# Layer 0's gates, branch and output projections as three products of high and low halves

## The reference

```python
def merge_branches(o_na, o_hg, hg_gate, gate_na, gate_hg, hg_gain, w_na_o, w_hg_o, w_out):
    y_na = from_heads(o_na) @ w_na_o
    y_hg = gated_head_norm(o_hg, hg_gate, hg_gain) @ w_hg_o
    return (jax.nn.sigmoid(gate_na) * y_na + jax.nn.sigmoid(gate_hg) * y_hg) @ w_out

# in parallel_mixer, for latent and context rows alike
(na_q, na_k, na_v, hq, hf, hb, hi, hg, ga, gh) = split_columns(h @ w_in)   # ga, gh: the two gates, 1024 columns each
# in reference, per layer
x = x + g1 * y_lat                                 # residual with the output projection
f = grouped_moe(...)                               # 16 experts, top-2 inside the best of 4 groups
```

## Time and profile before

| | |
|---|---|
| time, median of 3 runs | 1708.45 us (1707.89 to 1711.21) |
| the profiled execution's own time | 1708.12 us |
| its span | 1706.3 us |
| PE busy | 1538.7 us (90%) |
| DVE busy | 765.9 us (45%) |
| ACT busy | 571.5 us (33%) |
| POOL busy | 233.4 us (14%) |
| mean granted clock of the PE | 0.956 of full speed |

### The profile page before, as it was taken

The page is one execution under the profiler, slowest core; times in us unless marked ns, Lnnn a source line. Parts: engine busy times, 40 slices in busy tenths (PEclk is TensorE's granted clock), DMA queues, the critical chain, the costliest instruction groups (busy, mean ns, idle before and its releaser), DMA issues.

```text
span 1706.3 us, 15944 instructions
## 1 busy us (share of the span) xinstructions
PE 1538.7 (90%) x6246; PEld 913.2 (54%) x6246; DVE 765.9 (45%) x1047; ACT 571.5 (33%) x759; POOL 233.4 (14%) x204
## 2 busy tenths in 40 slices
PE   3999999999999995999999739999988996999885
PEld 1444665454444433788888525466547884443332
DVE  3045871666101125888888551665283114111103
ACT  3223431354000115787877442232142013111101
POOL 0005962200000001111110010074310000000000
PEclk9999999999999996999999959999998998999998
DMA  9411106498122223899999921112661445999992
GB/s 360 173 50 50 40 13 191 156 386 302 49 99 99 99 74 148 290 397 401 400 398 401 349 98 57 42 51 81 166 247 48 150 148 187 395 393 395 395 393 85
DMA packets 167139, 352.05 MB, mean 206 GB/s; under 512 B 21776, under 2 KB 22928, under 8 KB 167056
## 3 DMA queue, kind: packets, MB, share of 16 engines
q1 hardware_dynamic: 145472, 331.52, 52.2%
q0 software_dynamic: 3456, 12.58, 2.0%
q10 hardware_dynamic: 18128, 6.82, 2.0%
HBM read 339.38 MB, written 11.53 MB: 206 GB/s over the span
## 4 chain that ended last, share of the span: by engine, by line
PE 83%; DVE 6%; DMA 3%; issue 3%; ACT 2%; POOL 1%; SPq 0%; DVEq 0%; POOLq 0%; ACTq 0%
PE bank L501 20%; PE bank L512 6%; PE bank L1007 6%; PE bank L554 5%; PE bank L703 5%; PE bank L691 5%; PE bank L1029 4%; PE bank L790 3%; PE bank L784 3%; PE bank L781 3%; PE bank L578 2%; PE bank L472 2%; PE bank L814 2%; PE bank L1040 2%; PE bank L819 2%
## 5 line engine op out<-in xcount | busy, mean ns | idle before, releaser
L501 PE MATMUL bank<-hT,ring 128*128 128x512 f32 (+1 forms) x1024 | 371.1, 520 | 11.5 <-ACT hT L1330 6.4
L501 PEld LDWEIGHTS bank<-hT,ring 128*128 128x128 f32 x1024 | 197.0, 193 | 179.9 <-issue 160.7
L2233 DVE TENSOR_TENSOR slab_lo<-slab,high 128x4096 fp32r<-128x4096 f32 x48 | 212.0, 4420 | 6.8 <-ACT high L1517 6.2
L1517 ACT ACTIVATE high<-slab 128x4096 fp32r<-128x4096 f32 x48 | 174.1, 3632 | 23.0 <-PE bank L790 13.1
L1007 PE MATMUL bank<-narrow_slab,picked 128*64 128x512 f32 x256 | 114.4, 600 | 11.6 <-issue 11.4
L1778 POOL DMA_INDIRECT feed_rows<-token_table,slot_token x16 | 42.0, 2628 | 555.5 <-DVE slot_token L2173 360.5
L1008 PE MATMUL bank<-narrow_slab,picked 128*64 128x512 f32 x256 | 114.6, 601 | 0.0
L512 PE MATMUL bank<-ring,hT 128*128 128x512 f32 x256 | 110.5, 592 | 0.0
L554 PE MATMUL bank<-hT,ring 128*128 128x512 f32 (+1 forms) x256 | 104.8, 548 | 0.0
L1485 ACT ACTIVATE gsig<-bank 128x512 f32<-128x512 f32 (+1 forms) x32 | 15.7, 491 | 214.9 <-PE bank L501 214.9
L703 PE MATMUL bank<-merged,ring 128*128 128x512 f32 (+1 forms) x256 | 83.1, 486 | 2.6 <-DVE merged L2094 2.6
(11 more groups left out here) (260 smaller groups left out, 2249.2 us busy)
## 6 DMA issues: line engine op xcount, KB each, us to landing
ring<-in_w_ada SPq DMA_DIRECT2D x24, 2048.0 KB, 15.7
ring<-in_w_in SPq DMA_DIRECT2D x24, 2048.0 KB, 9.2
slab<-in_w_gate SPq DMA_DIRECT2D x16, 2048.0 KB, 14.7
slab<-in_w_up SPq DMA_DIRECT2D x16, 2048.0 KB, 14.9
slab<-in_w_down SPq DMA_DIRECT2D x16, 2048.0 KB, 14.7
narrow_slab<-in_w_gate SPq DMA_DIRECT2D x16, 2048.0 KB, 18.0
narrow_slab<-in_w_up SPq DMA_DIRECT2D x16, 2048.0 KB, 22.0
narrow_slab<-in_w_down SPq DMA_DIRECT2D x16, 2048.0 KB, 19.3
```

The costliest lines, as they stand in the source:

```text
L501: mm = T.matmul(o[:, lo:TOK], w[:, k, c * P:(c + 1) * P], hT[:, k, lo:TOK], start=(k == 0), stop=(k == KT - 1))
L1517: S.activation(high[kind][:], w[:], ACT.Copy)\
L2233: V.tensor_tensor(low[:], w[:], high[kind][:].bitcast(f32), ALU.subtract)\
```

## The change

In layer 0 the operands of the gate, branch and output projections are split into a high half (a copy to float32r, on ACT) and a low half (the rest, on DVE), and each float32 matmul becomes three float32r ones. Layer 1 keeps the old code.

- Weights are split by chunks of 128 output columns: `gate_high(n)`/`gate_low(n)` (1024 elements a row), `way_high`/`way_low` for the branches (512), `out_high`/`out_low` (1024). The high halves have two buffers of each kind; the low half overwrites the chunk in its ring slot.
- `hT` is split during attention: high halves of tiles 2 to 7 on ACT in steps p = 4 to 9, low halves over `hT` itself on DVE in steps 6 to 11; tiles 0 and 1 after attention. `ona`, `oh` and `merged` are split likewise.
- The head norm is taken in among the gates: the four sums (`head_squares`) stand between the PE's first products, the roots get four buffers (`ors`, `ors_more`), and DVE scales one head in each of the steps n = 1 to 4.
- The first two output chunks are prepared in steps 14 and 15; the rest beside the output projection.
- The fill of gate 0's slab waits for all 16 merges instead of the first, since its place now holds high halves.

The core of the diff (of `way_high`, `out_high`, `way_low`, `out_low` and `merged_high` only the use is shown; they are built as `gate_high` and `gate_low` are, a chunk waiting for the product that read its buffer two chunks before):

```diff
-merged = fixed("merged", [P, KT, TOK], offset=B0)
+merged = fixed("merged", [P, KT, TOK], offset=A0 + 32 * KB)
+ors_more = fixed("ors_more", [P, 2, TOK], offset=B0 + 36 * KB)
+hT_hi = fixed("hT_hi", [P, KT, TOK], f32r, offset=B0)
+hT_lo = fixed("hT_lo", [P, KT, TOK], f32r, offset=hT_at)
+ona_lo = fixed("ona_lo", [P, 4, TOK], f32r, offset=A0 + 24 * KB)
...
+gate_hi = [fixed(f"gate_hi{i}", [P, KT, P], f32r, offset=B0 + (24 + 4 * i) * KB) for i in range(2)]
+way_hi = [fixed(f"way_hi{i}", [P, 4, P], f32r, offset=B0 + (32 + 2 * i) * KB) for i in range(2)]
+out_hi = [fixed(f"out_hi{i}", [P, KT, P], f32r, offset=A0 + (16 + 4 * i) * KB) for i in range(2)]
...
+def gate_chunk(n):
+    br, d = n // KT, n % KT
+    key = ("in", 0, (8, 10)[br] + d // 4)
+    return key, chunk_of(slot(key), KT, d % 4), chunk_of(slot_low(key), KT, d % 4), gate_hi[n % 2]
+def way_chunk(n):
+    br, d = n // KT, n % KT
+    key = (("nao", "hgo")[br], 0)
+    return key, chunk_of(slot(key), 4, d), chunk_of(slot_low(key), 4, d), way_hi[n % 2]
...
+def wide_gates():
+    first = [2, 3, 4, 5, 6, 7, 0, 1]
+    for n in range(16):
+        br, d = n // KT, n % KT
+        key, _, low, high = gate_chunk(n)
+        o = open_bank(key + (d % 4,), "gate_sig")
+        pe.wait_ge(sem["chunk_high"], n + 1)
+        for i, k in enumerate(first):
+            if n == 0 and k in (2, 0):
+                pe.wait_ge(sem["tile_high"], (8, 0, 6)[k])
+            T.matmul(o[:, :], high[:, k, :], hT_hi[:, k, :], start=(i == 0), stop=False)
+        for i, k in enumerate(first):
+            if n == 0 and k in (2, 0):
+                pe.wait_ge(sem["tile_low"], (8, 0, 6)[k])
+            T.matmul(o[:, :], high[:, k, :], hT_lo[:, k, :], start=False, stop=False)
+        pe.wait_ge(sem["chunk_low"], n + 1)
+        for k in range(KT):
+            mm = T.matmul(o[:, :], low[:, k, :], hT_hi[:, k, :], start=False, stop=(k == KT - 1))
+        mm.then_inc(sem["psum_ready"], 1)
+        if d % 4 == 3:
+            slot_spent[slot_of(key)] = (sem["psum_ready"], jobs[0])
+        if n == 0:
+            head_squares(0)
+            head_squares(1)
+        key, _, low, high = way_chunk(n)
+        x_hi, x_lo = ((ona_hi, ona_lo), (oh_hi, oh_lo))[br]
+        o = open_bank(("y", l, br, d), "merged_ready")
+        pe.wait_ge(sem["way_high"], n + 1)
+        if d == 0:
+            pe.wait_ge(sem["head_high"], 4 * br + 4)
+        for k in range(4):
+            T.matmul(o[:, :], high[:, k, :], x_hi[:, k, :], start=(k == 0), stop=False)
+        if d == 0:
+            pe.wait_ge(sem["head_low"], 4 * br + 4)
+        for k in range(4):
+            T.matmul(o[:, :], high[:, k, :], x_lo[:, k, :], start=False, stop=False)
+        pe.wait_ge(sem["way_low"], n + 1)
+        for k in range(4):
+            mm = T.matmul(o[:, :], low[:, k, :], x_hi[:, k, :], start=False, stop=(k == 3))
+        mm.then_inc(sem["psum_ready"], 1)
+        if d == KT - 1:
+            slot_spent[slot_of(key)] = (sem["psum_ready"], jobs[0])
+        if n == 0:
+            head_squares(2)
+            head_squares(3)
+def wide_out():
     for d in range(KT):
+        key, _, low, high = out_chunk(d)
+        o = open_bank(("out", l, d), "x_updated")
+        pe.wait_ge(sem["chunk_high"], 16 + d + 1)
+        def by_high(ks, start):
+            for k in ks:
+                if d == 0:
+                    pe.wait_ge(sem["tile_high"], KT + k + 1)
+                T.matmul(o[:, :], high[:, k, :], merged_hi[k // 4][:, k % 4, :],
+                         start=(start and k == 0), stop=False)
+        def by_low(ks):
+            for k in ks:
+                T.matmul(o[:, :], low[:, k, :], merged_hi[k // 4][:, k % 4, :],
+                         start=False, stop=False)
+        def rest(ks):
+            for k in ks:
+                if d == 0:
+                    pe.wait_ge(sem["tile_low"], KT + k + 1)
+                mm = T.matmul(o[:, :], high[:, k, :], merged_lo[:, k, :],
+                              start=False, stop=(k == KT - 1))
+            return mm
+        parts = (range(KT - 1), range(KT - 1, KT)) if d == 0 else (range(KT),)
+        for n, ks in enumerate(parts):
+            by_high(ks, n == 0)
+            pe.wait_ge(sem["chunk_low"], 16 + d + 1)
+            by_low(ks)
+            mm = rest(ks)
+        mm.then_inc(sem["psum_ready"], 1)
+        if d % 4 == 3:
+            slot_spent[slot_of(key)] = (sem["psum_ready"], jobs[0])
...
         elif i == LANE[GATE][0]:
-            sp.wait_ge(sem["merged_ready"], 1)
+            sp.wait_ge(sem["merged_ready"], 16)
...
+def keep_hT_high(k):
+    if k == 2:
+        act.wait_ge(sem["bias_ready"], NA_HEADS)
+    elif k == 0:
+        act.wait_ge(*is_ready(("TR", 0, 2 * len(pairs) - 1)))
+    S.activation(hT_hi[:, k, :], hT[:, k, :], ACT.Copy).then_inc(sem["tile_high"], 1)
+def gate_high(n):
+    if n >= 16:
+        return
+    key, w, _, high = gate_chunk(n)
+    if n % 4 == 0:
+        act.wait_ge(*full(key))
+    if n >= 2:
+        act.wait_ge(*is_ready(gate_chunk(n - 2)[0] + ((n - 2) % 4,)))
+    S.activation(high[:], w, ACT.Copy).then_inc(sem["chunk_high"], 1)
...
+    keep_hT_high(0)
+    keep_hT_high(1)
+    act.wait_ge(sem["na_z"], 2 * len(pairs))
+    gate_high(0)
+    way_high(0)
+    act.wait_ge(*is_ready(("PV", 0, len(pairs) // 2 - 1)))
+    act.wait_ge(sem["oh_ready"], 4)
+    square_head(0)
+    square_head(1)
+    act.wait_ge(sem["na_o"], len(pairs) // 2)
+    for h in range(4):
+        S.activation(ona_hi[:, h, :], ona[:, h, :], ACT.Copy).then_inc(sem["head_high"], 1)
+    gate_high(1)
+    way_high(1)
+    for h in range(HG_HEADS):
+        head_std(0, h, 0)
+        if h + 2 < HG_HEADS:
+            square_head(h + 2)
+    for n in range(16):
+        gate_sigmoid(n)
+        gate_high(n + 2)
+        if n > KT:
+            merged_high(n - 1 - KT)
+        way_high(n + 2)
+        if n == 6:
+            act.wait_ge(sem["og_ready"], 4)
+            for h in range(4):
+                S.activation(oh_hi[:, h, :], oh[:, h, :], ACT.Copy).then_inc(sem["head_high"], 1)
+        if n >= 14:
+            out_high(n - 14)
+    merged_high(KT - 1)
...
+    if l == 0 and 4 <= p < 10:
+        keep_hT_high(p - 2)
...
+def low_half(low, x, high, done):
+    V.tensor_tensor(low, x, high.bitcast(f32), ALU.subtract).then_inc(sem[done], 1)
+def keep_hT_low(k):
+    dve.wait_ge(*is_ready(("in", 0, 7, 3)))
+    dve.wait_ge(sem["tile_high"], [2, 3, 4, 5, 6, 7, 0, 1].index(k) + 1)
+    low_half(hT_lo[:, k, :], hT[:, k, :], hT_hi[:, k, :], "tile_low")
+def gate_low(n):
+    if n < 16:
+        _, w, low, high = gate_chunk(n)
+        dve.wait_ge(sem["chunk_high"], n + 1)
+        low_half(low, w, high[:], "chunk_low")
...
+    if l == 0 and 6 <= p < 12:
+        keep_hT_low(p - 4)
...
+def wide_gates():
+    keep_hT_low(0)
+    keep_hT_low(1)
+    gate_low(0)
+    way_low(0)
+    for h in range(4):
+        dve.wait_ge(sem["head_high"], h + 1)
+        low_half(ona_lo[:, h, :], ona[:, h, :], ona_hi[:, h, :], "head_low")
+    gate_low(1)
+    way_low(1)
+    for n in range(16):
+        merge(n)
+        gate_low(n + 2)
+        if n > KT:
+            merged_low(n - 1 - KT)
+        way_low(n + 2)
+        if 1 <= n <= HG_HEADS:
+            scale_head(n - 1)
+        if n == 6:
+            for h in range(4):
+                dve.wait_ge(sem["head_high"], 4 + h + 1)
+                low_half(oh_lo[:, h, :], oh[:, h, :], oh_hi[:, h, :], "head_low")
+        if n >= 14:
+            out_low(n - 14)
+    merged_low(KT - 1)
...
+    if l == 0:
+        out_low(d + 2)
```

169 lines of the change are left out of this document (121 added, 48 removed).

## The result

The changed kernel takes 1663.95 us (median of 4 runs, 1657.18 to 1664.72), beside 1708.17 us for the kernel before on the same chip (4 runs, 1707.41 to 1711.21). The ratio is 0.9732, with a 95% interval of 0.9711 to 0.9754. In a second group the same kernel took 1661.67 us (5 runs) against 1707.7, ratio 0.9722 [0.9706, 0.9738]. The forecast was 1659.4 with 1650 to 1666 as its range. So the sign and the size are right, and 2 to 5 us of the gain are missing.

The account below looks back on a forecast made before the run. PE alone was taken to bound the changed stage. Products 45.1, attention's edge 1.7 and the output projection's edge 2.0 sum to 48.8 us off 1708.12, giving 1659.3, stated as 1659.4 us; range 1650 to 1666.

Parts of the forecast that it names:

- The products: Gates, branches, output projection: 219.8 us of float32 records replaced by 768 float32r products at 0.2275, 174.7 us; 45.1 us gained.
- The upper bound: Price of a float32r product: at most the experts' 0.2275 us, since that holds under far more traffic.
- Rival A: Changed stage: products run at the float32 passes' pace, 0.2147 us; 58.6 us gained, 1649.5 us; chance 0.09.
- The edge at attention's end: From attention's last values into the gates: beside the products it costs 3.7 instead of 5.4 us; 1.7 us gained.
- The edge to the output projection: Between last branch matmul and output projection: the gap behind the last merge goes; 2.0 us gained.
- The loop: 15 further gate and branch tiles: PE's 8.19 us a tile hides ACT and DVE (at most 7.4); nothing charged.
- rival B: Attention's end, steps 1 to 4 and attention: halves come late and PE stands; 5 us lost, 1664; chance 0.13.
- Attention: Low halves and roundings of hT added to attention's steps: charged at 0, upper end 4.1 us.
- The queues: Ring and slab fills: gate 0's fill starts at 543.9, first used 67 us later; nothing charged.
- rival C: Layer 0's experts: DMA stream sets their end and starts late; 9.6 us slower, 1718; chance 0.02.
- Rival D: Changed stage: splitting keeps pace at PE's cost and nothing is left, within 0.2%; chance 0.01.
- Behind the stage: From the norm on: everything moves as a whole; the clock's return may shift a us or so each way.

Follow-up runs that it names:

- e5: Changed kernel with the whole block of tiles from hT_hi on, and those behind it, moved up 192 bytes to lie like the others: 1659.79 us, ratio 0.971.
- e10: Changed kernel with input high halves, weight high halves and ors_more moved 192 bytes, the block behind kept in place within 256 bytes: 1662.19 us in one profile.
- e4: Changed kernel with each low half of a weight chunk made twice on DVE, first into a scratch tile: 1665.21 us, ratio 0.9748.
- e11: Changed kernel with gate and branch weight halves nearly unmade on ACT and DVE after two chunks, third product reading high halves: 1662.79 us in one profile.
- e1: Changed kernel with layer 0's output projection back as float32 matmuls, without halves for it: 1677.61 us, ratio 0.9814.
- e3: Changed kernel without the product of weights' low halves with inputs' high halves; all halves still made and waited for: 1601.26 us, ratio 0.938.
- e6: Kernel before the change, with only the fill of gate 0's slab waiting for all 16 merges: 1708.84 us, ratio 1.0005.
- the control: The changed kernel run again without an edit, beside the kernel before: 1661.67 us, 5 runs from 1657.09 to 1666.92.
- e2: Changed kernel with almost no low halves of weights made (one column in 128), third product reading the high half instead: 1662.6 us, ratio 0.9727.
- e9: Changed kernel with only the block behind the input halves (osq, ors, gsig, gmul, square, normed) moved 192 bytes: 1660.31 us in one profile.

## Why the forecast came out as it did

**The products.** Mechanism right, size off. The mis-sized term was 768 x 0.2275 = 174.7 us. 192 of the products, in the output projection, cost 0.2267, 0.15 us less in all. The other 576 cost 0.2325, because the new tiles were laid 64 bytes off the others: 576 x 0.005 = 2.9 us over the term. With the tiles alike they cost 0.2267 too, and e5 and e10 give back 3.1. I had named this point as one where I might be wrong (another price than the experts' show), but my bounds were 0.2147 and 0.2275, and the value lay above both. The upper bound rested on traffic, of which the experts have far more; e4 and e11 show that DVE's and ACT's traffic does not set this price. What the experts' rows had in common with each other, and not with the new tiles, was the placement, and I never compared the addresses in the diff. Had I done so, no row of before would have priced the difference, but the upper bound would have been left open.

**Rival A** did not come true. The gates' and branches' float32r products with all tiles alike, no idle time and a clock of 1.00 (e5, e10) start 0.2267 us apart, not 0.2147; why the difference stays is open. The Trainium skill's rule (TensorE: Matmul & The Clock Gate, "Wait — 56ns, not 53.3ns?"), 215.7 ns for 512 columns, does not hold for these products: the measured value decides.

**The edge at attention's end.** Forecast 1.7 us gained; measured 0.5 better than that. ACT was earlier than I had it: it rounded `hT` behind its own last copy and not behind the values.

**The edge to the output projection.** 2.0 us gained as forecast, and e1 brings 1.7 of it back.

**The loop and rival B.** DVE and ACT cost nothing: no wait of PE in the loop, and e4, with the weights' low halves made twice, costs half a us, all in the first tile. My bound of 0.8 us of slack (7.4 against 8.2) was too careful, for the reason that e3 shows: a rate above PE's for four tiles only uses up the lead.

**Attention.** Charged at 0, and from its first scores to its last values, 321.7 to 404.41 us, it is as long as before, from 323.0 to 405.74.

**The queues and rival C.** Charged at 0; e6 shows nothing from a fill that comes 46 us later. Rival D fell with the result.

**Behind the stage.** Here the forecast said that things move as a whole, and that the clock may shift a us or so each way. It was 4.8 us in the profiled run, all one way. It goes with the clock that PE is granted. In layer 0's experts, the first 30 us have a mean of 0.94 before and 0.85 after. The window of the kernel before:

```profile
682.66:713.00 30.34, 28.55 (x127) 23.39 (x128) 25.13 (x20) 21.64 (x15) 3.30 (x3) 0.94 0.72 256
```

The same stretch of the changed kernel:

```profile
634.72:665.00 30.28, 28.51 (x117) 23.09 (x117) 23.89 (x20) 19.17 (x13) 1.37 (x2) 0.85 0.66 228
```

The products behind a pause, from PE's timeline, first in the trace of before:

```profile
700.06 2.12 PE L784 MATMUL bank<-high,feed_lo 128*128 128x512 f32 x8 [1.79 <-DVE feed_lo L2240]
```

And in that of the changed kernel:

```profile
652.92 3.06 PE L913 MATMUL bank<-high,feed_lo 128*128 128x512 f32 x8 [1.77 <-DVE feed_lo L2528]
```

Both kernels pause for 1.8 us in this stretch (PE is busy 28.5 of 30.3 us in each). After the pause eight products of the changed kernel take 655.78 - 652.92 = 2.86 us at a mean granted clock of 0.65, in place of 702.02 - 700.06 = 1.96 at 1.00. Another 0.8 us is lost earlier. The experts' first eight products take 3.55 us, 0.44 each, in both kernels, that is, at the lower level of the clock. The next eight take 640.98 - 638.27 = 2.71 us in the changed kernel and 688.15 - 686.21 = 1.94 before: the clock comes back later there. In front of layer 1's experts PE's timeline shows the router's products, the same code in both kernels. In the trace of before:

```profile
1414.27 4.89 PE L716 MATMUL bank<-hT,router 128*16 128x256 f32 x16 [3.54 <-ACT hT L1330]
```

And in that of the changed kernel:

```profile
1368.10 6.52 PE L845 MATMUL bank<-hT,router 128*16 128x256 f32 x16 [3.54 <-ACT hT L1461]
```

Is this the change's doing? The twelve profiles of the experiments say not in a fixed way. Layer 0's experts take 288.2 to 289.6 us in ten of them, the control's 289.38 among them, and 291.4 in e2 and e1. These two and the changed kernel's first profile are also the only ones in which the clock falls behind that pause: the row of its eight products is 2.7 to 3.2 us long there and 2.1 in all others. The router's products take 6.5 us in the control and e10, 4.9 to 5.0 in e2 and e9. So a run falls on one side or the other at each of these pauses, at the first of them with the very same kernel. Whether the changed kernel falls on the slow side more often than the one before is not shown. The control's runs lie between 1657.09 us at a mean clock of 0.959 and 1666.92 at 0.950; those of before in the same group between 1706.38 and 1710.59. By this spread a forecast for this kernel has an error of 2 to 5 us. What decides on which side a pause falls is open; I did not try to steer it.

**The two together** account for the profiled run: 48.8 forecast, less 2.1 in the stage (2.9 for the products of gates and branches; 0.5 given back at the first edge and 0.15 in the projection; the rest is rounding), less 4.8 for the clock, plus 1.33 upstream, plus 0.3 elsewhere, is 43.5.

The best version that leaves nothing out is the change with its tiles placed like the others (e5): 1659.79 us, 0.971 of the kernel before. Its advantage over the change itself is read from the profile; the timed intervals overlap. That its time is so near the forecast's 1659.4 is partly luck, since what the clock takes behind the stage was not in the sum.

## What to carry to other kernels

Where PE bounds a stage and a float32 matmul stands as two records of 0.43 us, three float32r products of high and low halves take 0.68 us in place of 0.86, and here the splitting was free, as it was done two tiles ahead; count the lead and not only the rate. Read the price of an instruction from rows whose operands also lie alike in memory, and lay new tiles at the same place within 256 bytes as the old ones; 64 bytes off is the one other place that was measured. And behind a pause of PE, untouched code kept its length in these profiles to no better than about 2 us a pause.

## What was not expected of the hardware

- The place of a product's operands: with tiles 64 bytes off each other a float32r product of 512 columns starts 0.2325 us after the last, with all alike 0.2267. A tile of 36 products takes 8.36 or 8.16 us. Moving weights or inputs alone gives 8.25 to 8.35. Halving ACT's work beside the products changes no tile behind the first by more than 0.01 us (e11 against e2).
- The clock behind a short pause: a pause of 1.8 us of PE was followed by products at 0.36 us in one trace (2.86 us for eight), and by products at the full clock in another of the same kernel (2.11 us for the row of eight in the control).
